# The recurrent tail of a two-block transformer kernel: numerators copied by ScalarE, denominators and norms in 32-row groups, a pipelined head loop

## The reference

```python
# mLSTM per direction, all positions at once in the kernel:
s   = (q . k) * exp(d_log - m_q)            # causal weights W
num = s @ v;   den = sum(s)
h   = num / max(|den|, exp(-m_q))
ml_h = h(forward) + h(backward)
# both groups:
y_gla = rmsnorm(gla_o, gla_g_norm) * silu(gla_gate)
y_ml  = sigmoid(ml_ogate) * rmsnorm(ml_h, mlstm_g_norm)
x = x + gt1 * (concat([y_gla, y_ml]) @ w_out)
# the decays of GLA and the forget gates of mLSTM, before that:
log_a = log_sigmoid(dec) / 16;   log_f = log_sigmoid(pre)
```

## Time and profile before

| | |
|---|---|
| median of three runs | 3111.82 us (3111.04 to 3112.64) |
| the profiled execution | 3113.84 us, its span 3112.1 us |
| TensorE busy, matmul / weight load | 93% / 86% of the span |
| VectorE, ScalarE busy | 63%, 47% |
| mean granted clock of TensorE | 0.964 |

### The profile page before, as it was taken

How to read it: one execution, slowest core, us unless ns; L and a number is a source line. 1 busy time by engine, 2 the same in 40 slices (tenths; PEclk the granted TensorE clock), 3 DMA queues, 4 the chain that set the end, 5 groups by cost and what they waited for, 6 DMA issues and landing times.

```text
span 3112.1 us, 52132 instructions
## 1 busy us (share of the span) xinstructions
PE 2905.8 (93%) x21018; PEld 2670.1 (86%) x21018; DVE 1970.3 (63%) x2763; ACT 1454.1 (47%) x1818; POOL 0.2 (0%) x4
## 2 busy tenths in 40 slices
PE   7899888999669899999999999999999799999978
PEld 4467555699569899999999999999999799988978
DVE  6755555568466777777655566667644687645575
ACT  6545444454333444444444555555433454455443
POOL 0000000000000000000000000000000000000000
PEclk9999999999889899999999999999999899999989
DMA  8655545643105345455555454545455254432433
GB/s 334 238 195 201 218 176 216 231 147 141 44 18 185 135 176 188 176 188 176 188 176 181 172 189 176 188 177 188 165 181 183 95 189 168 166 133 101 172 118 126
DMA packets 92251, 530.34 MB, mean 170 GB/s; under 512 B 8240, under 2 KB 8784, under 8 KB 34912
## 3 DMA queue, kind: packets, MB, share of 16 engines
q1 hardware_dynamic: 90752, 524.32, 46.1%
q10 hardware_dynamic: 1376, 4.27, 0.4%
HBM read 526.46 MB, written 2.10 MB: 170 GB/s over the span
## 4 chain that ended last, share of the span: by engine, by line
PE 68%; DVE 4%; ACT 1%; issue 1%; DMA 0%; DVEq 0%; ACTq 0%
PE ps L1527 21%; PE ps L1528 21%; PE ps L1529 21%; PE ps L1839 2%; PE ps L1976 1%; DVE ssq L883 0%; PE ps L1973 0%; ACT hi L436 0%; DVE lo L834 0%; PE ps L1817 0%; PE ps L1524 0%; PE ps L1526 0%; PE ps L1525 0%; DVE rden L1172 0%; PE ps L1576 0%
## 5 line engine op out<-in xcount | busy, mean ns | idle before, releaser
L834 DVE TENSOR_TENSOR lo<-raw,hi 128x1024 fp32r<-128x1024 f32 x700 | 853.4, 1224 | 683.1 <-ACT hi L436 681.6
L436 ACT ACTIVATE hi<-raw 128x1024 fp32r<-128x1024 f32 x700 | 736.6, 1057 | 891.4 <-PE ps L1529 879.7
L900 DVE TENSOR_TENSOR lo<-raw,hi 128x1024 fp32r<-128x1024 f32 x290 | 341.7, 1223 | 281.4 <-ACT hi L471 280.9
L471 ACT ACTIVATE hi<-raw 128x1024 fp32r<-128x1024 f32 x290 | 293.2, 1053 | 345.5 <-PE ps L1526 153.0
L1527 PE MATMUL ps<-x2h,hi 128*128 128x256 f32 x1376 | 391.9, 285 | 11.2 <-DVE x2l L845 11.2
L1529 PE MATMUL ps<-x2h,lo 128*128 128x256 f32 x1376 | 391.4, 284 | 0.0
L1528 PE MATMUL ps<-x2l,hi 128*128 128x256 f32 x1376 | 391.4, 284 | 0.0
L1527 PE MATMUL ps<-xph,hi 128*128 128x256 f32 x1024 | 290.9, 284 | 0.1
L1528 PE MATMUL ps<-xpl,hi 128*128 128x256 f32 x1024 | 290.3, 284 | 0.0
L1529 PE MATMUL ps<-xph,lo 128*128 128x256 f32 x1024 | 290.2, 283 | 0.0
L1527 PEld LDWEIGHTS ps<-x2h,hi 128*128 128x128 f32 x1376 | 266.3, 194 | 12.4 <-issue 11.2
(11 more groups left out here) (373 smaller groups left out, 6968.1 us busy)
## 6 DMA issues: line engine op xcount, KB each, us to landing
raw<-in_weights SPq DMA_DIRECT2D x491, 1024.0 KB, 4.8
xf<-in_xt SPq DMA_DIRECT2D x8, 512.0 KB, 9.7
raw<-in_weights SPq DMA_DIRECT2D x4, 768.0 KB, 4.6
R<-in_xt ACTq DMA_DIRECT2D x1, 2048.0 KB, 8.5
out<-R SPq DMA_DIRECT2D x1, 2048.0 KB, 6.3
maskn<-in_maskn ACTq DMA_DIRECT2D x1, 512.0 KB, 3.5
ptr<-in_pt ACTq DMA_DIRECT2D x2, 256.0 KB, 3.6
vec<-in_vec ACTq DMA_DIRECT2D x1, 411.5 KB, 5.2
```

The lines of the kernel that those rows point to most:

```text
L436: act.activation(HI[p % PAIR][:, c], RAW[p % RING][:, c], ACT.Copy).then_inc(hi_ready, 1)
L471: act.activation(half_of(HI, u), RAW[t % RING][:, h * SLOT // 2:(h + 1) * SLOT // 2], ACT.Copy).then_inc(hi_ready, 1)
L834: dve.tensor_tensor(LO[p % PAIR][:, c], RAW[p % RING][:, c], HI[p % PAIR][:, c].bitcast(F32), ALU.subtract).then_inc(lo_ready, 1)
L900: dve.tensor_tensor(half_of(LO, u), RAW[t % RING][:, h * SLOT // 2:(h + 1) * SLOT // 2], half_of(HI, u).bitcast(F32), ALU.subtract).then_i ...
```

## The change

1. **Front.** ScalarE's Exp and Ln of the decays and of the forget-gate rows are pinned to slot `+ 2` behind their value slot, not `+ 1`. VectorE's part stays.
2. **Row repetition.** The eight repeated rows are now 256 columns wide in four banks, with four copies; the stabilisers are repeated by two matmul pairs straight into 32-row groups (`four`), one partition group of 32 for each of four weight steps, and copied to `em`.
3. **GLA outputs** are copied from banks 0 to 3 by ScalarE to `yg` beside the squares. The scores may start after these copies (`gla_evac`); no norm stands before the head loop.
4. **32-row groups.** `onew` is 224 columns of zeros with ones in columns 96 to 127, so that a window of 128 columns puts a sum in one 32-row group of the result. Four weight steps accumulate their denominators in bank 6, and one maximum, one absolute value and one reciprocal serve all four. Sums of squares go the same way (`group_sums`). `group_rep` brings a group back to all 128 partitions: one matmul with a repeated column of `eye` for each group.
5. **Head loop.** Three buffers of `wgt`; weights of step n+2 are prepared during step n; ScalarE copies the numerators out of bank 4+d (`num_evac`) to `ym` and `num1`. The GLA norm and gates, and the denominators of heads 0 and 1, are placed between steps on all three engines. Those of heads 2 and 3 follow the loop.
6. `yf` is gone: `yg` and `ym` are gated in place. `R` is loaded after the GLA copies rather than before the loop.

The core of the diff (buffer addresses, the unchanged bodies of moved operations and removed lines that repeat are left out):

```diff
-                    if n == AT["value", 2 * m] + 1:
+                    if n == AT["value", 2 * m] + 2:
...
-                if n == AT["value", 8] + 1:
+                if n == AT["value", 8] + 2:
...
-            for n in range(8):
+            for n in range(4):
...
+                act.activation(neg_g[:, n * 512:(n + 1) * 512], PS[(7, 2, 0, 1)[n]][:, :], ACT.Copy).then_inc(sem("rep_ready"), 1)
...
+            def weights(n):
...
+                W = wgt[n % 3]
+                if n >= 3:
+                    act.wait_ge(sem("ml_done"), n - 2)
...
+                    act.activation(W[:, t * T:(t + 1) * T], blk(neg_g, 4 * d + h), ACT.Exp, bias=gtok[:, c:c + 1]).then_inc(sem("w_ctx"), 1)
+                act.wait_ge(sem("w_arg"), n + 1)
+                act.activation(W[:, 0:2 * T], W[:, 0:2 * T], ACT.Exp).then_inc(sem("w_x"), 1)
...
+            weights(0)
+            for p in range(2):
+                act.wait_ge(sem("row_rep"), 5 + p)
+                act.activation(em[p][:, :], PS[4 + p][:, 0:T], ACT.Copy).then_inc(sem("em_ready"), 1)
+            weights(1)
             for h in range(HEADS):
...
-                act.activation(blk(osq, 2 * h, 2), PS[h][:, :], ACT.Square).then_inc(sem("gla_sq"), 1)
...
+                act.activation(blk(yg, 2 * h, 2), PS[h][:, :], ACT.Copy).then_inc(sem("gla_evac"), 1)
+                act.activation(blk(osq, 2 * h, 2), PS[h][:, :], ACT.Square).then_inc(sem("gla_evac"), 1)
+            act.dma_start(R[:, :], A["xt"][:, 0:KD * T]).then_inc(sem("R_loaded"), 16)
...
+            for n in range(8):
+                if n + 2 < 8:
+                    weights(n + 2)
+                if n == 2:
+                    act.wait_ge(sem("gla_sum"), 1)
+                    act.activation(rgla[:, :], PS[7][:, 0:T], ACT.Sqrt, bias=v("eps"), scale=1.0 / DV).then_inc(sem("gla_root"), 1)
+                if n == 6:
+                    ml_squares(0)
+                    ml_squares(1)
+                if n == 7:
+                    ml_root(0, 7)
+                act.wait_ge(sem("ml_done"), n + 1)
...
+                act.activation(blk((ym, num1)[d], 2 * h, 2), PS[4 + d][:, :], ACT.Copy).then_inc(sem("num_evac"), 1)
+            y_hi(0)
+            y_hi(1)
+            ml_squares(2)
+            ml_squares(3)
+            ml_root(1, 2)
+            y_hi(2)
+            y_hi(3)
...
+            def weight_arg(n):
...
+                if n >= 3:
+                    dve.wait_ge(sem("ml_done"), n - 2)
...
+            def denominators(p):
+
+                dve.wait_ge(sem("ml_done"), 4 * p + 4)
...
+                den, r = PS[6][:, 0:T], rden[p][:, :]
+                own.done(dve.tensor_tensor(r, den, em[p][:, :], ALU.max))
+                own.wait()
+                dve.scalar_tensor_tensor(r, den, -1.0, r, ALU.mult, ALU.max).then_inc(sem("den_taken"), 1)
+                dve.wait_ge(sem("den_taken"), p + 1)
+                dve.reciprocal(r, r).then_inc(sem("rden_ready"), 1)
+
+            def both_directions(h, bank):
+
+                dve.wait_ge(sem("den_rep"), h + 1)
...
+                for d, t in ((0, ym), (1, num1)):
+                    a = blk(t, 2 * h, 2).rearrange("p (a t) -> p a t", t=T)
+                    own.done(dve.tensor_tensor(a, a, PS[bank][:, d * T:(d + 1) * T][:, None, :].to_broadcast([P, 2, T]), ALU.mult))
+                own.wait()
+                dve.tensor_tensor(blk(ym, 2 * h, 2), blk(ym, 2 * h, 2), blk(num1, 2 * h, 2), ALU.add).then_inc(sem("ml_h"), 1)
...
+            weight_arg(0)
+            weight_arg(1)
+            dve.wait_ge(sem("gla_out"), 4)
+            own.done(dve.memset(onew[:, :], 0.0))
+            own.wait()
+            dve.memset(onew[:, 96:128], 1.0).then_inc(sem("onew_ready"), 1)
+            for n in range(8):
+                weight(n)
...
+                    weight_arg(n + 2)
+                if n == 2:
+                    dve.wait_ge(sem("gla_root"), 1)
+                    dve.reciprocal(rgla[:, :], rgla[:, :]).then_inc(sem("rgla_ready"), 1)
+                if n == 3:
+                    dve.wait_ge(sem("gla_rep"), 1)
+                    gated_y(yg, "gla_g", 0, 0, 7)
+                if n == 4:
+                    denominators(0)
+                    dve.wait_ge(sem("gla_rep"), 2)
+                    gated_y(yg, "gla_g", 0, 1, 7)
+                if n == 5:
+                    both_directions(0, 7)
+                if n == 6:
+                    both_directions(1, 7)
+                if n == 7:
+                    norm_recip(0)
+            denominators(1)
+            dve.wait_ge(sem("norm_rep"), 1)
+            gated_y(ym, "ml_g", 8, 0, 7)
+            both_directions(2, 0)
+            both_directions(3, 1)
+            y_rest(0)
+            norm_recip(1)
+            y_rest(1)
+            dve.wait_ge(sem("norm_rep"), 2)
+            gated_y(ym, "ml_g", 8, 1, 3)
+            y_rest(2)
+            y_rest(3)
...
+            def group_sums(o, squares, sem_name):
...
+                for j, sq_ in enumerate(squares):
+                    for a in range(2):
+                        ins = pe.matmul(o, onew[:, 96 - 32 * j:224 - 32 * j], sq_[:, a * T:(a + 1) * T], start=j + a == 0,
+                                        stop=j == len(squares) - 1 and a == 1, skip_group_check=True)
+                ins.then_inc(sem(sem_name), 1)
...
+            def group_rep(bank, groups, src, sem_name):
+
+                for i, j in enumerate(groups):
+                    ins = pe.matmul(PS[bank][:, i * T:(i + 1) * T], eye[:, 32 * j:32 * j + 1].to_broadcast([P, P]), src[:, :],
+                                    start=True, stop=True, skip_group_check=True)
+                ins.then_inc(sem(sem_name), 1)
...
+            for p in range(2):
+                pe.matmul(PS[4 + p][:, 0:T], four[p][:, :], rowh[:, T:2 * T], start=True, stop=False, skip_group_check=True)
+                pe.matmul(PS[4 + p][:, 0:T], four[p][:, :], rowl[:, T:2 * T], start=False, stop=True, skip_group_check=True).then_inc(sem("row_rep"), 1)
+            pe.wait_ge(sem("rep_ready"), 4)
             gla_outputs()
...
+                if h < 2:
+                    pe.wait_ge(sem("gla_evac"), 4 * h + 4)
...
+            def ml_step(n):
...
+                pe.wait_ge(sem("ml_w"), n + 1)
+                if n >= 2:
+                    pe.wait_ge(sem("num_evac"), n - 1)
+                else:
+                    pe.wait_ge(sem("em_ready"), n + 1)
...
+                if n == 4:
+                    pe.wait_ge(sem("den_taken"), 1)
+                for t in range(4):
+                    ins = pe.matmul(PS[6][:, 0:T], onew[:, 96 - 32 * j:224 - 32 * j], W[:, t * T:(t + 1) * T], start=j + t == 0,
+                                    stop=j == 3 and t == 3, skip_group_check=True)
+                ins.then_inc(sem("ml_done"), 1)
...
+            for n in range(8):
+                ml_step(n)
+                if n % 2 == 0 and n < 6:
+                    ml_scores(n // 2 + 1)
+                if n == 1:
+                    pe.wait_ge(sem("gla_evac"), 8)
+                    group_sums(PS[7][:, 0:T], [blk(osq, 2 * h, 2) for h in range(HEADS)], "gla_sum")
+                if n == 2:
+                    pe.wait_ge(sem("rgla_ready"), 1)
+                    group_rep(7, (0, 1), rgla, "gla_rep")
+                if n == 3:
+                    pe.wait_ge(sem("operand_made"), reached("made", "y", 1))
+                    group_rep(7, (2, 3), rgla, "gla_rep")
+                if n in (4, 5):
+                    pe.wait_ge(sem("rden_ready"), 1)
+                    pe.wait_ge(sem("operand_made"), reached("made", "y", 2))
+                    if n == 5:
+                        pe.wait_ge(sem("ml_h"), 1)
+                    group_rep(7, (2 * (n - 4), 2 * (n - 4) + 1), rden[0], "den_rep")
+                if n == 6:
+                    pe.wait_ge(sem("ml_h"), 2)
+                    pe.wait_ge(sem("ml_sq"), 2)
+                    group_sums(PS[7][:, 0:T], msq, "ml_sum")
+            pe.wait_ge(sem("rml_ready"), 1)
+            group_rep(7, (0, 1), rml[0], "norm_rep")
+            pe.wait_ge(sem("rden_ready"), 2)
+            for h in (2, 3):
+                group_rep(h - 2, (2 * (h - 2), 2 * (h - 2) + 1), rden[1], "den_rep")
+            pe.wait_ge(sem("ml_sq"), 4)
+            group_sums(PS[2][:, 0:T], msq, "ml_sum")
+            pe.wait_ge(sem("rml_ready"), 2)
+            group_rep(3, (0, 1), rml[1], "norm_rep")
```

240 lines of the change are left out of this document (89 added, 151 removed).

## The result

The changed kernel takes 3042.8 us (median of 4 runs, 3042.1 to 3044.5); the kernel before took 3111.4 us beside it (3109.1 to 3112.6). The ratio is 0.9778 with a 95% interval of 0.9766 to 0.9791, so 68.6 us are gone. The forecast was 3047 us. The profiled execution has a span of 3040.3 us, 71.8 less than before.

A forecast was written before the change was run, and what follows sets the result against it. TensorE, busy nine tenths of the span, was taken as the bound, with waits worth having in front and tail. Front 24.4 plus tail 40.1 made 64.5 us, taking the median of 3111.82 to 3047; range 3036 to 3064.

The forecast's parts named there:

- The front, first two pairs: Behind value slots 0 and 2: TensorE's 2.72 us waits go to zero and the clock recovers, 11.9 us together.
- The front, third and fourth pair and forget gates, the idle time: Behind value slots 4, 6 and 8: waits shrink to 2.67, 2.67 and 2.1 us, gaining 4.47, 4.47 and 3.6.
- the first rival: Waits behind value slots 4, 6, 8 move rather than vanish; front gains only 12 us, 3060 us; chance 0.10.
- the estimate that was 1.6 us higher: Front, ScalarE's block: with the skill's 2.66 us table switch it is 2.8 us longer, raising the estimate 1.6 us.
- The front, the clock behind these waits: Behind value slots 4, 6 and 8: remaining waits of 2.67 and 2.1 us still drop TensorE's clock.
- the upper bound of 30: Front: gain of 30 us if the three remaining waits no longer drop the clock, some 1.7 us each.
- The tail: Row repetition to `mix_out`: shorter repetition, a loop without waits and a VectorE chain behind it, 40.1 us gained.
- The cover in the loop: Head loop, end of step 3 to step 5: VectorE's 7.6 us of work fits in 8.6.
- The second rival: VectorE bounds the head loop; steps 3 to 6 start 2 to 3 us late, 14 us, 3061; chance 0.09.
- Sum: Whole kernel: front 24.4 plus tail 40.1, 64.5 us saved, median 3047; nothing behind `mix_out` touched.

The follow-up runs named there:

- tail alone: The changed kernel with ScalarE's Exp and Ln blocks back at their old slot ends, new tail kept: 3070.6 us, ratio 0.9861.
- twice repeated: The changed kernel with each repetition of a GLA norm or denominator inside the head loop made twice: 3046.6 us, slower by 3.8.

## Why the prediction was right, point by point

- **The front, first two pairs.** Forecast 11.9; at 351.73 the changed trace is 11.98 us ahead (363.71 less 351.73). Right against this execution of the kernel before; "tail alone" shows that 2.2 us of it were the clock of that execution (it has the same two waits and is 2.25 us ahead at 361.46), so the closeness is in part luck.
- **The front, third and fourth pair and forget gates, the idle time.** Forecast 2.67 left behind slots 4 and 6, 2.1 behind 8, gains 4.47 each and 3.6. Measured 2.62, 2.61 and 2.06, so 4.52, 4.53 and 3.68, with `lo` as the releaser. Right. ScalarE's block did not hold the next modulation half, and the first rival (3060) is out. The table loads took 1.28 us and the activation followed at once (374.93 plus 1.28, next start 376.22). The drain that the Trainium skill states (ScalarE: Activation LUTs, What ACT_TABLE_LOAD costs) shows in no row, and with it goes the estimate that was 1.6 us higher.
- **The front, the clock behind these waits. This is the term that was off.** The forecast priced "2.67 us of idle time stay, with the drop of the clock as before", and for the forget gates "I take the drop". In the changed trace the drops did not come: 1.00 behind all three. In the kernel before they had cost 1.3 us behind 391, 1.7 behind 438 and 2.3 behind 485 us (growth of the lead between the waits, less the idle time saved), 5.3 together. That is the difference between 24.4 and 30.6 but for 0.9, of which 0.6 are shorter falls behind the two waits of 3.6 us; the upper bound of 30 had been worked out for just this case. The step that failed is reading a yes or no from one row each: 2.72 had fallen, 1.77 had not, so 2.67 and 2.1 were given the drop. Eight traces say that behind 2.6 us it falls in two executions of eight, and behind 2.06 us at this place in none. In those two the front gives 28.6 and 29.2 us instead of 30.6.
- **The tail.** Forecast 40.1 from row repetition to `mix_out`; measured 40.1. On the clock of the trace before (add 30.56): step 0 at 801.5 (forecast 801.3), last denominators 856.9 (856.6), two heads combined 866.2 (866.3), norm sums done 870.8 (870.5), `mix_out` 874.7 (874.6). Its parts are shown, not only their sum: TensorE's 0.43 us by "twice repeated" (the matmuls that it adds are those with a repeated column of `eye`), the waits behind the loop by the trace. The terms are off by up to 0.3 us and partly cancel; that the sum agrees to 0.1 is luck, that the terms do is not. Of the changes in the tail, the GLA norm in the loop (some 10 us) and the third buffer (some 20) have runs of their own, whose gains overlap; the 32-row groups and the early copies have none, so what each of these is worth is not shown.
- **The cover in the loop.** "The margin of 1 us in steps 4 and 5 is thin": in the trace after, the weights product of step 5 ends at 807.1 and the step starts at 808.17, so 1.0 us, as worked out. It held, since the durations of the operations there came out as in the rows; 7.2 us more on VectorE took 1.0 us beyond it. The second rival (3061) is out.
- **Sum.** 24.4 + 40.1 = 64.5 was forecast; 30.56 + 40.05 + 1.2 = 71.8 of the span and 68.6 of the medians were measured. Of the span's miss of 7.3 us, 6.2 lie in the front, 5.3 of them the clock behind the three waits, and 1.2 behind `mix_out`. The medians miss by only 4, since the profiled execution of the kernel before was 2.4 us above its median and that of the changed kernel 0.7 below.

## What to carry to other kernels

Where three engines feed each other in order, pinned side work costs what stands ahead of the operand wanted next. List at each slot end what TensorE still has in hand, and put the side work where that is a whole value half rather than a few short modulation halves; moves of one slot end each gave 29 us in the change and 19 more in two further versions (some 2 of them luck), without an instruction less. In a chain such as sum, root, reciprocal, repetition, look for other work to put between the links on TensorE, and for a third buffer where the queue that refills it also carries other work: with two, not the weights came late but everything behind them. Price a clock drop behind a wait of 2 to 3 us as a chance, not as a yes or no, and look for it in a window of several us behind the wait, not in the first matmul.
